# A hybrid attention and expert layer: the loops of TensorE's program in both expert stages written out

## The reference

```python
def peer(h, w_query, sub_keys, expert_u, expert_v):
    q = (t @ w_query).reshape(n_tok, PEER_HEADS, 2, PEER_HALF)
    s = jnp.einsum('thcd,hcnd->thcn', q, sub_keys)
    v1, i1 = lax.top_k(s[:, :, 0], PEER_TOPK)
    v2, i2 = lax.top_k(s[:, :, 1], PEER_TOPK)
...
    u_sel = expert_u[ec]
    a = jax.nn.gelu(jnp.einsum('cd,chkd->chk', tc, u_sel), approximate=False)
    w = gc * a
    return jnp.einsum('chk,chkd->cd', w, expert_v[ec])
```

## Time and profile before

| | us |
|---|---|
| median of 3 runs (lowest, highest) | 1953.23 (1952.56, 1955.71) |
| the profiled execution's own time | 1951.24 |
| its span, first to last instruction | 1949.3 |
| PE busy | 1940.0 (100%) |
| PE weight loads busy | 1765.4 (91%) |
| DVE busy | 1664.4 (85%) |
| ACT busy | 1122.1 (58%) |
| POOL busy | 664.4 (34%) |

### The profile page before, as it was taken

How to read it: one execution, slowest core, us unless ns; L and a number is a source line. 1 busy time by engine, 2 the same in 40 slices (tenths; PEclk the granted TensorE clock), 3 DMA queues, 4 the chain that set the end, 5 groups by cost and what they waited for, 6 DMA issues and landing times.

```text
span 1949.3 us, 32645 instructions
## 1 busy us (share of the span) xinstructions
PE 1940.0 (100%) x11722; PEld 1765.4 (91%) x11722; DVE 1664.4 (85%) x2523; ACT 1122.1 (58%) x1589; POOL 664.4 (34%) x409
## 2 busy tenths in 40 slices
PE   9999999999999999999999999999999999999999
PEld 8899989998988888999999999999888888888887
DVE  8777778777888777999999999998888988888887
ACT  7565556555677455656665665655555455555555
POOL 0301110011000001887777877686222221333220
PEclk9999999999999999999999999999999999999999
DMA  6745654565455556999999999999999999999997
GB/s 246 252 160 194 204 191 159 188 204 194 162 173 192 185 173 228 336 341 341 334 334 341 345 326 355 336 384 356 358 364 387 381 374 371 381 376 381 371 379 270
DMA packets 137575, 566.50 MB, mean 291 GB/s; under 512 B 44008, under 2 KB 52080, under 8 KB 88112
## 3 DMA queue, kind: packets, MB, share of 16 engines
q1 hardware_dynamic: 87152, 414.05, 58.1%
q0 software_dynamic: 49936, 149.49, 22.9%
q10 hardware_dynamic: 432, 2.37, 0.3%
HBM read 548.31 MB, written 16.88 MB: 290 GB/s over the span
## 4 chain that ended last, share of the span: by engine, by line
PE 90%; DMA 4%; DVE 3%; ACT 1%; issue 1%; DVEq 0%; ACTq 0%; SPq 0%
PE psum L946 25%; PE psum L923 16%; PE psum L616 15%; PE psum L928 10%; PE psum L620 8%; PE psum L602 3%; PE psum L601 3%; PE psum L606 3%; DMA raw<-v_rows 2%; DMA arena<-u_cols 1%; ACT whi L479 1%; DVE xr L487 1%; DVE wlo L487 1%; PE psum L818 1%; PE psum L1000 0%
## 5 line engine op out<-in xcount | busy, mean ns | idle before, releaser
L473 DVE TENSOR_TENSOR wlo<-raw,whi 128x1024 fp32r<-128x1024 f32 x242 | 296.1, 1231 | 110.3 <-PE psum L620 72.2
L923 PE MATMUL psum<-xr,whi 128*128 128x384 f32 x2048 | 380.9, 337 | 0.0
L946 PE MATMUL psum<-whi,xr 128*128 128x512 f32 x1512 | 364.0, 390 | 0.3 <-DVE xr L1888 0.2
L923 PEld LDWEIGHTS psum<-xr,whi 128*128 128x128 f32 x2048 | 351.2, 188 | 0.5 <-ACT whi L479 0.2
L946 PEld LDWEIGHTS psum<-whi,xr 128*128 128x128 f32 x1512 | 283.6, 188 | 60.4 <-ACT whi L479 1.0
L479 ACT ACTIVATE whi<-raw 128x2048 fp32r<-128x2048 f32 x168 | 320.9, 1910 | 27.5 <-DMA raw<-v_rows 17.0
L616 PE MATMUL psum<-xr,whi 128*128 128x512 f32 x1296 | 330.2, 397 | 0.0
L466 ACT ACTIVATE whi<-raw 128x1024 fp32r<-128x1024 f32 x244 | 250.4, 1054 | 110.7 <-DMA raw<-stream 52.9
L1388 POOL DMA_INDIRECT arena<-v_rows,small x64 | 142.2, 2222 | 399.5 <-DVE arena L1852 396.0
L616 PEld LDWEIGHTS psum<-xr,whi 128*128 128x128 f32 x1296 | 232.6, 189 | 43.6 <-issue 0.2
L487 DVE TENSOR_TENSOR wlo<-raw,whi 128x1024 fp32r<-128x1024 f32 (+1 forms) x126 | 197.6, 1573 | 23.4 <-issue 19.9
(11 more groups left out here) (283 smaller groups left out, 3236.4 us busy)
## 6 DMA issues: line engine op xcount, KB each, us to landing
raw<-stream SPq DMA_DIRECT2D x244, 512.0 KB, 3.3
raw<-v_rows SPq DMA_DIRECT2D x85, 1024.0 KB
raw<-u_cols SPq DMA_DIRECT2D x84, 1024.0 KB
arena<-v_rows SPq DMA_DIRECT2D x43, 1024.0 KB, 7.9
arena<-u_cols SPq DMA_DIRECT2D x42, 1024.0 KB, 6.8
gates<-arena POOLq DMA_DIRECT2D x8, 1536.0 KB, 9.7
small<-gates SPq DMA_DIRECT2D x62, 192.0 KB, 8.2
arena<-x_t SPq DMA_DIRECT2D x4, 544.0 KB, 6.6
```

Of the source, the lines that this page charges most:

```text
L473: nc.vector.tensor_tensor(wlo[:, k % 2 * HALF:(k % 2 + 1) * HALF], raw[:, s * HALF:(s + 1) * HALF], f(whi[:, s * HALF:(s + 1) * HALF]), AL ...
L923: mm(bank(at, 0, 2 * TD), hi_w[:, c * P:(c + 1) * P], z_all[:, :, c, 0:TD // TS, :], start=c == 0, stop=False)
L946: last = mm(at[:, (b * 4 + j * 2 + n) * 512:(b * 4 + j * 2 + n + 1) * 512], weights, src, start=begin, stop=end, skip_group_check=True)
```

## The change

PE's two loops in the expert stages become Python loops, which write all blocks into PE's program; `base` is a constant then. Block `b` of the score stage still uses bank and weight half `b % 4`, and value blocks 2 to 122 are one range.

```diff
-            with pe.Fori(0, B_U // 4 - 1) as i:
-                for q in range(4):
-                    expert_block(i * 4 + F_U, 4 + q, q)
+            for b in range(4, B_U):
+                expert_block(F_U, b, b % 4)
...
-            with pe.Fori(0, B_V // 2 - 4) as i:
-                for q in range(2):
-                    value_block(i * 2, 2 + q, False)
-            value_block(0, B_V - 6, False)
+            for c in range(2, B_V - 5):
+                value_block(0, c, False)
```

## The result

| | before | changed |
|---|---|---|
| median, us (lowest, highest; runs) | 1954.01 (1948.31, 1958.12; 22) | 1957.70 (1953.02, 1965.85; 22) |
| ratio of the two, 95% interval | | 1.0026 [1.0019, 1.0034] |
| the profiled execution's own time, us | 1951.24 | 1956.15 |

The changed kernel is slower by 0.26%: the medians are 3.7 us apart, the means 5.0. The predicted time, 1953.7 us, is 4 us short of the measured one. "The same" was the forecast, and the measured median is just past the 1957.1 us from which the prediction called a result slower.

The account below looks back on a forecast made before the run. PE's own stream was taken to bound both expert stages, with DMA at 0.97 next. Terms 0 + 0.5 + 0 on the median 1953.23 gave 1953.7 us; range 1949.5 to 1958.8.

Parts of the forecast that it names:

- The same: Forecast case for the whole kernel: measured time between 1949.3 and 1957.1 us, not told from no change; chance 86%.
- Turns and register work: PE's loops in both stages: removing 91 turns and the register instructions saves 0, between -1.7 and +1.7 us.
- Code, added: PE's code queue q8, both stages: 51 more packets, about 32 and 19 by stage; PE's wait 0, at most 3.1 us.
- the first rival: Written-out stages: PE waits for code at each 16 KB boundary, 49 us if all are exposed, 2002 us; chance 7%.
- Late weight loads, +0.5 us: Value stage: code packets make two weight loads land too late for ACT's copies, 0.25 us each, +0.5 us.
- The clock: Whole span: granted clock 1.00 throughout, the 2.4 GHz level, so a changed clock can't come into it.
- Waits, reordered: Block starts in both stages: with constants hi_done stands ahead in PE's issue, still met 2.02 us before use; cost 0.
- issue held at `hi_done`: Slower rival, value blocks: PE needs over 2.02 us after that wait; at 0.1 us over, 12 us, 1965.7 us; chance 2%.
- the Trainium skill's branch rule: Taken branches leave the fetched window and stall; cited under the faster rival at loop turns, 87 us, 1866 us, chance 1%.
- ACT's wait for `v_rows` well over 17 us: Sign of a wrong forecast, value stage: this wait, with late PE starts beside q8 packets, means the 0.5 us was too small.
- within 2 us: Sign of a right forecast: the score and value stages stay this near to 588 and 574 us.

Follow-up runs that it names:

- short turns: Kernel before, its loop bodies lengthened to 12 score blocks (ten turns) and 20 value blocks (six turns): 1952.61 us, 1.0002.
- swapped loops: Kernel before, loops kept, the two waits at a block's start swapped so that hi_done stands ahead of the first matmul: 1953.47 us, 0.9997.
- the halves: Kernel before with half of each stage written out: next to the stages' border (inner) 1956.63 us, 1.0018; away from it (outer) 1954.36 us, 1.0013.
- Long turns: Kernel before, its loop bodies lengthened to 60 blocks, two turns in each stage: 1972.04 us, 1.0099.
- middle bodies: Kernel before, its loop bodies lengthened to 24 score blocks (five turns) and 40 value blocks (three turns): 1987.27 us, 1.0189.
- double dose: Kernel before, loops kept, plus 103 unread DRAM copies of 256 KB, every second score block and every third value block: 1960.90 us, 1.0033.

## Why the prediction was wrong

**Turns and register work, 0: right.** The beat is 4.573 and 4.533 us before and after, short turns (16 turns for 91) and swapped loops stand within their interval of the kernel before. The price that was weighed there, an estimated 9.8 us from the 108 ns of a compare-and-branch in the Trainium skill, "Advanced Engine Details and Errata", Control Flow Timing, is nowhere in the time: removing 91 of them brought nothing.

**Code, added: the count right, PE's own wait right.** 49 packets came for the 51 forecast, and 31 between 800 and 1360 us for about 30; most of the blocks at which one comes keep the beat, so the first rival (code late at each 16 KB) doesn't occur.
The Trainium skill, "Runtime: NRT & Kernel Launch", Instruction fetch mechanics, has this fetch mostly hidden: for PE the trace agrees. That the loads beside it pay, the page doesn't say.

**Late weight loads, +0.5 us: this is the step that failed.** The whole change measures 4.5 ± 1.1 us over all runs, and the other terms next to nothing, so this one was too small by a factor of nine; it comes to about 4.5 / 49 = 0.09 us a packet. Three things in its working were wrong:
- "With 19 packets over 126 blocks": only the value stage was counted. The score stage gets 31 packets, and there ACT's waits rose by 10 us in the change's profile, at the copies next to a packet.
- "Another 0.96 on one DMA engine makes 1.8, which is still covered": the mean wait was set against the slack. Lateness is made by the tail: ACT waited 3.40 us before the copy at 1289.07, where the mean wait for a `raw` load is 21.7 / 21 = 1.0. The slack itself was right: 3.40 - 2.02 = 1.38 us are left of that wait, and the block was 1.42 late. Delay beyond the slack goes to PE in full.
- A late block was charged once, at 0.25 us. In the changed trace single blocks were late by 0.77 and 1.42 us, and the block behind such a one is often a little late as well.

What the runs put in its place: with DMA engines busy 0.97 of the time, code packets of 16 KB make some weight loads of the score stage land late. Shown are that written-out code costs 4.5 us, and 3.6 with the other order of waits; that held loops with the same blocks cost nothing; that in the score stage ACT waits longer for loads at the copies next to a code packet, and not at the others; and that foreign copies in PE's looped program cost 2.6 us at 51 times 256 KB and 7.6 at 103. In the change's profile PE then waits for ACT's copies, and less for DVE's rests; in its two repetitions it waits more for the rests (1.1 against 2.2 us, 0.7 against 2.0). Not shown is how one packet does it: the trace doesn't tell which DMA engine took it. If a load of 1 MB counts as landed only when its last part is there, one held-up engine could be as bad as sixteen, and 49 packets could match 51 copies of sixteen; this is argued only. Nor do the profiles hold all of the 4.5 us: the three of the change ran 1956.15, 1954.41 and 1953.90 us, all below the mean of its runs, 1958.2. And lateness scatters from one execution to the next: values alone, with the loops kept in the score stage, lost 10.6 us in that stage in its first profile, and 2.0 and 4.8 in the other two.

**The range.** The measured time lies inside it, by luck. Its upper end, 1958.8, was made by adding 3.1 us for PE waiting at code packets, which isn't what happened; without them it would have been 1955.7.

**The clock.** That a changed clock "can't come into it" was said too firmly, since in some executions the granted clock is 0.998 or 0.999 as a mean: 7 of 46 runs of the change, 8 of the 148 of the kernel before that were taken beside the experiments. It isn't the cause either. In the runs at 1.000 the means are 1957.4 and 1953.4 us, still 4.0 apart.

**Waits, reordered, 0: right but for a little.** Swapping them changes nothing that can be told in either kernel; at late copies the order adds 0.1 us.

**The rivals.** None occurred. The slower ones had other mechanisms (PE waiting for code, issue held at `hi_done`), and the result came out slower by the term that the forecast held too small; to any slower result, by other mechanisms, it had left 9%.
What was said there of the Trainium skill's branch rule was too broad. Its section has a branch stall when its target lies outside the two fetched blocks; counting a matmul as two instructions, the looped bodies of 128 and 40 matmuls fit into two blocks of 256 (an estimate), and of the rows only the loop over heads, with 448 matmuls and no q8 row, speaks against the rule.
The section on what would show it named the true sign, ACT's wait for `v_rows` well over 17 us (it was 25.0) with late PE starts; that it stood there and not in the sum is the error. That reading alone would have misled, since the runs show the score stage's waits to be the ones that follow the packets. The stages, 3.0 and 2.5 us longer, also miss the "within 2 us" that was named there for a right forecast.

**Open.** The stages don't add up: 1.3 ± 1.1 and 0.2 ± 1.0 alone, 4.5 ± 1.1 together, 3.0 ± 1.8 more than the sum. So the late loads of the score stage are shown, but most of the cost appears only when the value stage is written out too, and its cause is open. Lateness carried across the border of the stages, or packets of the score stage that cost only with those of the value stage, would do it; the halves, 3.9 ± 1.5 and 2.0 ± 1.9 on their chip, don't decide. No kernel tried beats the one before.

## What to carry to other kernels

A loop whose body the engine held cost nothing here, on an engine that is fed ahead; writing it out bought nothing, and added one code packet of 16 KB for every 16 KB of code to what DMA carries. Where DMA is near its limit and the bounding engine waits for loads, price an added packet by the tail of the load waits (the longest ones against the slack), not by their mean or by the share of bandwidth alone. Effects of a few us need dozens of runs of both kernels, and a half that shows nothing alone isn't free for that.

## What the runs showed that was not expected

**A jump back to code no longer held is dear.** Long turns (q8 72 packets, for the 60 expected), PE in order of time at the jump of the score stage:

```profile
1067.81 1.50 PE L928 MATMUL psum<-xr 128*128 128x192 f32 x12
1074.30 3.83 PE L923 MATMUL psum<-xr,whi 128*128 128x384 f32 x13 [4.99 <-issue]
1079.85 0.69 PE L923 MATMUL psum<-xr,whi 128*128 128x384 f32 x3 [1.72 <-issue]
```

Busy times of the stretch before the jump and the one after it; the last three columns are granted clock, DMA share and GB/s:

```profile
1060.00:1069.00 9.00, 9.00 (x65) 9.00 (x64) 9.00 (x22) 4.69 (x5) 6.94 (x4) 1.00 0.94 340
1069.00:1083.00 14.00, 7.29 (x40) 6.98 (x40) 6.17 (x16) 2.79 (x4) 8.34 (x6) 0.88 0.93 325
```

And the code queue in the second stretch:

```profile
q8 instruction: 3, 0.05, 1.3%
```

PE stands 4.99 us and then 1.72 us with nothing but issue to wait for, while three packets come one after another (at 1071.7, 1077.5 and 1081.4 us); that block and the next are late by 5.15 + 3.27 = 8.4 us. With the middle bodies it happened at four turns of the score loop, 5.0 to 8.5 us each. The middle bodies' trace, the stretch after such a jump and its first rows on PE:

```profile
906.00:915.00 9.00, 6.28 (x28) 6.29 (x28) 5.30 (x6) 0.00 (x0) 7.72 (x5) 0.62 0.92 305
908.72 5.22 PE L923 MATMUL psum<-xr,whi 128*128 128x384 f32 x16 [4.96 <-issue]
```

After 4.96 us of idle PE the granted clock is 0.62 as a mean of 9 us: for 6.8 us it was at 0.5, the 1.2 GHz level, and 16 matmuls took 5.22 us instead of 2.97. So part of the price is the clock.

**A late block can cost the clock too.** In the double dose, PE at the latest block:

```profile
1287.06 4.56 PE L923 MATMUL psum<-xr,whi 128*128 128x384 f32 x16 [1.68 <-ACT whi L479]
1291.46 1.92 PE L928 MATMUL psum<-xr,wlo 128*128 128x192 f32 x16
1293.22 2.97 PE L923 MATMUL psum<-xr,whi 128*128 128x384 f32 x16
```

```profile
1286.00:1291.00 5.00, 3.94 (x14) 3.95 (x15) 3.96 (x4) 3.54 (x4) 2.10 (x3) 0.66 1.05 397
```

PE was idle for 1.68 us, the granted clock then stood at 0.5 for 3.4 us (0.66 over the 5 us of the window), and 16 matmuls took 4.56 us for 2.97. In one profile of the values alone the same followed an idle time of 1.43 us. After the 1.26 us of the changed kernel's worst block it did not: 3.02 us. The length of the idle time alone doesn't decide: in the middle bodies' value stage PE was idle for 2.46 us before 1584.12, and the clock stayed at 1.00. So a late load can cost PE more than its lateness (here 4.56 - 2.97 = 1.6 us more), which is a further reason to go by the tail.

**What PE holds.** Bodies of 384 and 400 matmuls jump back with no packet and no gap (short turns); a body of 768 doesn't, in four turns of four. A body of 800 matmuls in the value stage does both. At its first turn, the block at 1584.12 is 2.62 us late, with q8 packets at 1579.7, 1580.9, 1587.5 and 1594.4 us, and packets go on through that pass. The profile puts PE's wait there down to an ACT copy that ended at 1584.00, but that is the next block's; its own had ended at 1579.48. At the next turn the block is on the beat, and q8 has no packet in all of the third pass. Why the same body is fetched anew once and held once is open.
The Trainium skill, "Runtime: NRT & Kernel Launch", Instruction fetch mechanics, lets a branch out of the fetched blocks stall: true in the long and middle turns, and not in loops of up to 400 matmuls. The same section gives PE's store as 2048 instructions; a matmul counted as two, a body of 768 is an estimated 1536 and should fit, but it was fetched again at all four turns, and one of an estimated 1600 at one turn of two.
